# A pooling mixer's value and gate projections for groups 2 to 4 by seven block products, with weight sums made in DRAM

## What is computed

```python
def pool_mixer(h, w_in, w_grp, scale, w_out):
    v, gate = jnp.split(h @ w_in, 2, axis=-1)
    cs = jnp.cumsum(v32, axis=1)
    for g, w in enumerate(POOL_WINDOWS):          # windows 2, 4, 8, 16
        sl = slice(g * POOL_GROUP_DIM, (g + 1) * POOL_GROUP_DIM)
        ...
        groups.append((c - c_shift) / cnt - v32[..., sl])
    u = jnp.einsum('blgc,gcd->blgd', u, w_grp).reshape(b_, L, E_POOL) * scale
    return (u * jax.nn.silu(gate)) @ w_out
```

## Time and profile before

| | us |
|---|---|
| three runs: lowest, median, highest | 1538.06, 1538.21, 1538.75 |
| the profiled execution, its own time | 1539.07 |
| its span, first to last instruction | 1537.3 |
| PE busy | 1524.9 |
| DVE busy | 1049.2 |
| ACT busy | 577.6 |
| POOL busy | 362.9 |
| bytes moved by DMA | 170.75 MB |

### The profile page before, as it was taken

The page is one execution under the profiler, slowest core; times in us unless marked ns, Lnnn a source line. Parts: engine busy times, 40 slices in busy tenths (PEclk is TensorE's granted clock), DMA queues, the critical chain, the costliest instruction groups (busy, mean ns, idle before and its releaser), DMA issues.

```text
span 1537.3 us, 29781 instructions
## 1 busy us (share of the span) xinstructions
PE 1524.9 (99%) x12343; PEld 1366.5 (89%) x12343; DVE 1049.2 (68%) x1750; ACT 577.6 (38%) x1038; POOL 362.9 (24%) x333
## 2 busy tenths in 40 slices
PE   9999999999999999999999999999999999999998
PEld 9999999999998899889898898888888988888887
DVE  6656565765767678676887678779615787797246
ACT  5323222253344244434444445472112246541121
POOL 0000000030422134032332224434430044343510
PEclk9999999999999999999999999999999999999999
DMA  5322322323332324322334233554324335552331
GB/s 171 110 83 84 101 91 83 109 85 101 102 107 89 111 88 136 111 84 93 103 112 139 70 117 112 155 163 139 98 94 138 110 103 151 148 168 83 124 123 55
DMA packets 151859, 170.75 MB, mean 111 GB/s; under 512 B 6348, under 2 KB 122480, under 8 KB 151728
## 3 DMA queue, kind: packets, MB, share of 16 engines
q1 hardware_dynamic: 119728, 138.71, 29.0%
q10 hardware_dynamic: 31920, 29.97, 6.6%
q0 software_dynamic: 80, 0.20, 0.0%
HBM read 151.82 MB, written 17.04 MB: 110 GB/s over the span
## 4 chain that ended last, share of the span: by engine, by line
PE 48%; DVE 3%; ACT 0%; issue 0%; ACTq 0%
PE acc L415 13%; PE acc L416 13%; PE acc L417 13%; PE aux L417 1%; PE aux L416 1%; PE aux L415 1%; PE aux L1420 1%; DVE xns L2569 1%; PE aux L1438 1%; PE aux L1439 0%; PE aux L1386 0%; DVE yal L2559 0%; PE aux L643 0%; PE aux L645 0%; PE aux L576 0%
## 5 line engine op out<-in xcount | busy, mean ns | idle before, releaser
L415 PE MATMUL acc<-xhis,whi 128*128 128x264 f32 (+2 forms) x1848 | 608.9, 330 | 0.0
L417 PE MATMUL acc<-xhis,wlo 128*128 128x264 f32 (+2 forms) x1848 | 601.9, 326 | 0.0
L416 PE MATMUL acc<-xlos,whi 128*128 128x264 f32 (+2 forms) x1848 | 601.8, 326 | 0.0
L415 PEld LDWEIGHTS acc<-xhis,whi 128*128 128x128 f32 x1848 | 348.0, 188 | 29.8 <-issue 1.0
L417 PEld LDWEIGHTS acc<-xhis,wlo 128*128 128x128 f32 x1848 | 347.9, 188 | 29.3
L416 PEld LDWEIGHTS acc<-xlos,whi 128*128 128x128 f32 x1848 | 348.2, 188 | 27.1
L410 POOL TENSOR_TENSOR wlo<-raw,whi 128x1024 fp32r<-128x1024 f32 x84 | 208.5, 2483 | 366.0 <-DVE whi L2614 366.0
L406 ACT ACTIVATE whi<-raw 128x1024 fp32r<-128x1024 f32 x158 | 164.0, 1047 | 131.5 <-PE acc L417 119.3
L410 DVE TENSOR_TENSOR wlo<-raw,whi 128x1024 fp32r<-128x1024 f32 x81 | 99.8, 1235 | 36.9 <-ACT whi L406 36.7
L2292 DVE TENSOR_TENSOR wlo<-raw,whi 128x1024 fp32r<-128x1024 f32 x77 | 94.7, 1232 | 27.2 <-ACT whi L406 27.1
L2614 DVE CAST whi<-raw 128x1024 fp32r<-128x1024 f32 x84 | 61.2, 733 | 54.0 <-PE acc L417 53.8
(11 more groups left out here) (394 smaller groups left out, 2782.4 us busy)
## 6 DMA issues: line engine op xcount, KB each, us to landing
raw<-in_w_in SPq DMA_DIRECT2D x38, 1024.0 KB, 5.5
raw<-in_hgrn_w_in SPq DMA_DIRECT2D x32, 1024.0 KB, 5.9
raw<-in_pool_w_in SPq DMA_DIRECT2D x15, 1024.0 KB, 5.6
raw<-in_pool_w_out SPq DMA_DIRECT2D x8, 1024.0 KB, 4.9
raw<-in_hgrn_w_out SPq DMA_DIRECT2D x8, 1024.0 KB, 5.1
raw<-in_w_out SPq DMA_DIRECT2D x8, 1024.0 KB, 5.0
v_turn<-vb ACTq DMA_DIRECT2D x8, 544.0 KB, 2.7
raw<-in_pool_w_grp SPq DMA_DIRECT2D x4, 1024.0 KB, 5.3
```

Of the source, the lines that this page charges most:

```text
L415: pe.matmul(dst, stat[0], mov[0], start=first, stop=False)
L416: pe.matmul(dst, stat[0], mov[1], start=False, stop=False)
L417: return pe.matmul(dst, stat[1], mov[0], start=False, stop=last)
```

## The change

Groups 2 to 4 (G = 1 to 3) no longer make their four value and four gate units as such. Two units are taken together as a pair (p = 0, 1 the value pairs, p = 2, 3 the gate pairs). A pair's weight, 1024 x 256, is cut into four blocks of 512 x 128 (`d1`, `b12`, `d2`, `d3`), the input into four of 512 channels x 264 tokens. In place of the eight block products of a plain product there are seven, in Strassen's manner (Winograd's form): with `d1`, `d2`, `d3` and four sums of weight blocks, `t1 = d1 + b12`, `t3 = b12 + d3`, `t2 = d3 + t1`, `t4 = d2 + t2`. A block product is 4 tiles x 3 = 12 matmuls of 264 columns. Their results are accumulated in `aux`, `acc` and `aux2` and put together by small copies on ACT (`copied_sum`, 128 x 264, PSUM to `sqs`) and sums on DVE (`sum_11`, `sum_21`, `sums_2`, `scaled`).

- **Weight sums.** POOL issues, from its first us on, 8 DMAs per pair, DRAM to DRAM, 256 KB each: four copies, then four that accumulate, with a wait on `t_moved` after each of four steps. 12 pairs are made in 7 chains. SP waits for `t_moved` before it loads a chunk with such blocks.
- **Input sums.** Four sums of input blocks are made once: DVE's `s_sums` (8 operations, four times, after units 3 to 6 of group 1), split by ACT (`s_hi`) and DVE (`s_lo`).
- **Weight pieces.** For a pair there are 7 blocks of 128 x 512 to split, where there were 2 pieces of 128 x 1024. A `raw` chunk holds up to 4 blocks. `weight_blocks` makes the table of which block is split at which event, `weight_chunks` that of the loads.
- **Order.** In a group, the value pairs now come before the output units of the group before it; the gate pairs and the grp units come after these.

The core of the diff. The order of block products, and the chunks of weights:

```diff
+def strassen_order():
...
+    uses = []
+    for p in (0, 2):
+        uses += [(p, "d1"), (p, "d2"), (p, "t2"), (p, "t3"), (p, "d3"), (p, "t1")]
+        uses += [(p + 1, "d1"), (p + 1, "d2"), (p, "t4"), (p + 1, "t2"), (p + 1, "t3"), (p + 1, "d3"), (p + 1, "t1"),
+                 (p + 1, "t4")]
+    return uses
...
+def weight_chunks():
...
+    chunks = [("k8", 0, n) for n in range(4)] + [("k4", 0, 0)]
+    for G in range(1, NG):
+        chunks += [("blocks", G, (n, min(n + 4, 14))) for n in (0, 4, 8, 12)]
+        chunks += [("k4", G - 1, 1), ("k4", G - 1, 2)]
+        chunks += [("blocks", G, (n, min(n + 4, 28))) for n in (14, 18, 22, 26)] + [("k4", G, 0)]
+    return chunks + [("k4", NG - 1, 1), ("k4", NG - 1, 2)]
```

SP's waits before a chunk `c`:

```diff
+                    before, g, m = CHUNKS[c - RAW]
+                    if before == "blocks":
+                        wait_apart(sp, "sp", (sl_ready, N_USES * (g - 1) + m[1]))
+                    elif before == "k4":
+                        wait_apart(sp, "sp", (lo_ready, k4_piece(g, 2 * m + 2) + CREDIT))
...
+                if what == "blocks":
+                    sp.wait_ge(t_moved, T_MOVED[G, USES[n[1] - 1][0]])
```

POOL, right after its first memsets:

```diff
+            for G, pairs in T_CHAINS:
...
+                for p, (t1, t2, t3, t4) in zip(pairs, sums):
+                    pool.dma_start(t1, w_block(G, p, "d1")).then_inc(t_moved, 16)
+                    pool.dma_start(t3, w_block(G, p, "b12")).then_inc(t_moved, 16)
+                    pool.dma_start(t2, w_block(G, p, "d3")).then_inc(t_moved, 16)
+                    pool.dma_start(t4, w_block(G, p, "d2")).then_inc(t_moved, 16)
...
+                pool.wait_ge(t_moved, moved)
...
+                    pool.dma_start(t1, w_block(G, p, "b12"), accum_op=ALU.add).then_inc(t_moved, 16)
+                    pool.dma_start(t3, w_block(G, p, "d3"), accum_op=ALU.add).then_inc(t_moved, 16)
...
+                pool.wait_ge(t_moved, moved)
...
+                    pool.dma_start(t2, t1, accum_op=ALU.add, max_dma_last_dim=2048).then_inc(t_moved, 16)
...
+                pool.wait_ge(t_moved, moved)
...
+                    pool.dma_start(t4, t2, accum_op=ALU.add, max_dma_last_dim=2048).then_inc(t_moved, 16)
...
+                pool.wait_ge(t_moved, moved)
```

PE's order:

```diff
+            def two_units(G, p):
...
+                block_product(first, G, p, "d1", x_block(0, 0), True)
...
+                block_product(second, G, p, "d2", x_block(1, 0), True)
...
+                if p % 2:
+                    fourth_sum(G, p - 1)
...
+                pe.wait_ge(s_copied, 3 * t + 1)
+                block_product(first, G, p, "t2", s_block(1), False)
...
+                block_product(third, G, p, "t3", s_block(2), True)
...
+                pe.wait_ge(sum_done, summed(t, "11"))
...
+                block_product(second, G, p, "d3", s_block(3), True)
...
+                pe.wait_ge(s_copied, 3 * t + 2)
...
+                block_product(first, G, p, "t1", s_block(0), False)
...
+            for G in range(1, NG):
+                two_units(G, 0)
+                two_units(G, 1)
+                pe.wait_ge(sum_done, summed(4 * G - 3, "12"))
+                out_a_pair(G - 1)
+                fourth_sum(G, 1)
+                out_a(G - 1)
+                two_units(G, 2)
+                two_units(G, 3)
+                pe.wait_ge(sum_done, summed(4 * G - 2, "12"))
+                grp_a(G, 0)
+                fourth_sum(G, 3)
+                pe.wait_ge(sum_done, summed(4 * G - 1, "12"))
+                for n in range(1, GT):
+                    grp_a(G, n)
+            out_a_pair(NG - 1)
+            out_a(NG - 1)
```

DVE, the sums of input blocks, and their place in the loop over group 1's units:

```diff
+            def s_sums(k):
...
+                for half in range(2):
+                    dve.tensor_tensor(sq[half], xhi[:, 4 * half + k, :], xlo[:, 4 * half + k, :], ALU.add)\
+                       .then_inc(s_step, 1)
...
+                dve.tensor_tensor(s1, a22, a21, ALU.subtract).then_inc(s_step, 1)
+                dve.tensor_tensor(s2, a21, a22, ALU.subtract).then_inc(s_step, 1)
+                dve.tensor_tensor(s3, a11, a21, ALU.subtract).then_inc(s_step, 1)
+                dve.tensor_tensor(s4, a11, a12, ALU.subtract).then_inc(s_step, 1)
...
+                dve.tensor_tensor(s2, s2, a11, ALU.subtract).then_inc(s_step, 1)
+                dve.tensor_tensor(s4, s4, s1, ALU.add).then_inc(s_step, 1)
...
+                lows(("unit", u))
+                if 3 <= u < 7:
+                    s_sums(u - 3)
+                if 8 <= u < 12:
+                    s_lo(u - 8)
```

755 lines of the change are left out of this document (551 added, 204 removed).

## The result

| | before | changed |
|---|---|---|
| median of the runs (lowest, highest) | 1538.38 (1538.06, 1538.75), 4 runs | 1609.68 (1601.44, 1612.23), 4 runs |
| the profiled execution, its own time; its span | 1539.07; 1537.3 | 1601.44; 1598.9 |
| PE busy | 1524.9 | 1530.7 |

The ratio is 1.0451, with an interval of 1.0418 to 1.0484. The forecast was 1570, with a range of 1550 to 1600: the direction was right, the size was not, and the range did not hold it. The profiled execution is the fastest of the four, so the profile shows a loss of 61.6 us of span, and some 8 more are in the other executions, of which there is no trace.

A forecast was written before the change was run, and what follows sets the result against it. The prediction took PE's matmuls to bound the pooling mixer; 17.5 us saved against added waits, opening and contention gave +32.2 on 1539.07, 1571.3, or 1570 us beside the median, with a range of 1550 to 1600.

The forecast's parts named there:

- The pace, -17.5: Pooling mixer, PE: 144 matmuls fewer at 0.1213 us each, 17.5 us less, all on the path.
- Group 1, +9.8 and +3.9: Group 1: DVE's input sums delay evictions, PE loses 9.8 us; then t2 waits 3.9 us for ACT's copy of block 0.
- End of the value phase, +14.5: Groups 2 to 4, before output units: PE waits for sums_2 behind two landings in a row, 14.5 us.
- End of the gate phase, +6.9: Groups 2 to 4: PE's t4 of the fourth pair waits for sums behind the next group's first block, 6.9 us.
- start of the next value phase, +5.2: Groups 3 and 4: ACT's copy of the next block 0 comes 2.6 us after PE could use it, 5.2 us.
- last group, +1.4: Group 4: z_lo of the last grp unit stands behind a weight split, which the output units meet with 1.4 us.
- Opening, +2: Opening: POOL's first chain goes out beside the first inputs while PE waits for xt; 2 us, between nothing and 5.6.
- Contention, +6: 25 MB of sums until about group 4's end lengthen twelve landings on the path by 0.5 us each, 6 us.
- The clock: Rival: each of the five longest new waits brings 1.2 GHz for two block products, 14.5 us, 1585; chance 0.12.
- The loads keep up: Rival: weight chunks land before ACT asks, so the kernel is not slower, 1540 us or 1533; together 0.11.
- The sums come late: Rival: POOL's chains take 47 us, SP waits for t_moved, some 20 us over groups 3 and 4, 1590; chance 0.13.

The follow-up runs named there:

- small_s: Changed kernel with the input sums made over 8 or 16 columns instead of 264 or 528, every instruction kept: 1592.50 us.
- no_dma: Changed kernel without POOL's DMAs of weight sums, t1 to t4 loaded from plain weight blocks, no wait for t_moved: 1585.92 us.
- before_dma: Kernel before with POOL's 96 DMAs of weight sums added, whose results nobody uses or waits for: 1543.12 us.
- delay: Changed kernel with POOL's first chain sent after the input's last piece landed, and SP's t_moved wait naming the chunk's last pair with t blocks: 1595.48 us.
- holds: Kernel before with PE held up 18 times in groups 2 to 4 by waits for short POOL memsets: 1671.56 us.
- warm: Changed kernel with 24 matmuls on constants ahead of PE's wait before each group's first output pair: 1598.47 us.

## Why the prediction was right in direction and wrong in size

Step by step, with the terms as they were put.

**The pace, -17.5.** Holds: where the changed kernel has full clock and no wait, matmuls start 0.121 us apart as before, and there are 144 fewer.

**Group 1, +9.8 and +3.9.** The mechanism holds, the division doesn't. The sums took 3.55 us where 3.5 was worked out; the eviction behind them moved by 8.54, of which 5.0 is the opening. The first `pz` came 10.7 us late beyond the opening, but only 7.2 of these are waits of PE, less than forecast; 3.5 are slower matmuls, of which the forecast knew nothing. The last `pz`, forecast at 86.7, came at 91.7, which is exact beyond the opening's 5.0; as two errors met in it, that is partly luck. PE's wait for the first `t2` was 3.0, not 3.9. `small_s` gave 10 to 17 us back.

**End of the value phase, +14.5.** The mechanism holds row by row: copy behind `w_out` piece behind landing. It measured 21.5. Without the traffic it was 15.6 (`no_dma`), so the sum was right for landings without that traffic, and the landings with it were not.

**End of the gate phase, +6.9; start of the next value phase, +5.2; last group, +1.4.** The first was 9.6 with the traffic, 7.9 without; the two `t2` waits of groups 3 and 4 were 5.3 - 3.0 = 2.3, half of what was forecast; the grp units' waits for `zlos` 2.3. Another 5.2 us, for output units' evictions and the one without a releaser, have no term in the forecast.

**Opening, +2.** Mis-sized: 5.0 in the trace, and 4.4 alone (`before_dma`). The bound from above, 5.6, held. I had taken the low end on the argument that only four copies are out when PE waits. That was so, POOL issued the next step at 12.13 and PE's wait for `xt` ended at 12.34, but the four were enough: the wait grew by 3.4 us.

**Contention, +6.** Mis-sized too. I gave each of twelve landings 0.5 us. Between the profiled executions, up to the memset, the whole traffic is 15.0 us by `no_dma` and the opening's part 5.6 by `delay`, which leaves 9.4 for the landings behind it, where I had 6. The medians say 23.8 and 14.2 and leave the same; the 8 us more in both are the unexplained distance of the changed kernel's other executions. The median of the `w_out` landings grew by 1.0 us, and single ones by more: in group 2 a chunk was issued by 110.5 and ACT got it at 118.75, 8.3 us.

**The clock, nothing in the sum.** This is the step that failed. The forecast's waits came to 32.2 + 17.5 = 49.7 us; the new idle time is 54.8. Had the sum ended there it would have said 1576 for an execution that took 1601. (That the two sums of waits are so near is partly luck: the ends of the phases were too small in the forecast, group 1 and `t2` too large.) The missing 23.4 is PE's slower matmuls, 22.1 of them by the clock's record, and I had the clock as a rival at 0.12, because no row of the trace before showed a wait of 4 us or more. Even the rival was too small as put: it priced the five longest waits at 2.9 us each, 14.5. In fact `holds` shows 2.3 to 2.4 us for each wait of 4.80 us and more, and that waits of 2.48 us bring it in half of the cases. In the changed kernel's trace eleven of thirteen waits of over 1.5 us have a stretch of 0.50 within them or up to 1.4 us behind them, 2.0 us each. The rule of the Trainium skill ("TensorE: Matmul & The Clock Gate", Part 1), that the throttled clock is the default and only activity releases it, spoke for the rival, and the traces agree with it: the granted clock is 0.50 behind the waits in `holds`, and stays at 1.00 where `warm` keeps PE at work. With the 5.1 us that the waits were longer and the 23.4 of slower matmuls the sum would be 1571.3 + 5.1 + 23.4 = 1599.8, and that execution took 1601.4. The 8 us between it and the median stay open: other executions of the changed kernel may wait for longer landings, but none of them is in these rows.

The rivals otherwise. *The loads keep up* is refuted by ACT's 31.6 us of waits for `w_out`. *The sums come late* is refuted as well: POOL's DMAs of 512 rows followed each other by 0.61 to 0.65 us (once 0.77), not 2.8, so the issue is mostly a fixed cost, and the last of them went out at 253 us.

The other page that the prediction weighed, "DMA: Bandwidth & Descriptors" of the Trainium skill, gives its fit in the section on the anatomy of one DMA for DMAs that GpSimd issues; 4.4 us for 1 MB is my estimate from it. The loads in question are SP's, so the prediction used the fit outside of what the page states it for. Here it was 4.9 for `w_out` before, 5.2 in `no_dma` and 5.9 with the weight sums; the measured landings decide, and the estimate is below each of them.

## What to carry over

Sum the waits that a change brings to the engine on the path, and then add for each of them what the clock takes afterwards: here 2.3 to 2.4 us for each wait of 4.8 us and more and 1.7 us in half of the cases for one of 2.5 us, which made the difference between 2.4% and 4% in the profiled execution. A change that saves matmuls by giving other engines small, dependent work must leave slack at every handover, since a load that nobody waited for before turns all traffic, its own included, into time on the path. Traffic that costs little in one kernel (4.4 us here) is no measure of what it costs in another (15 to 24). And compare a trace with the time of its own execution first: the changed kernel's is 8 us off its median, as much as some of the effects read from it.

## What I had not expected of the hardware

- PE's granted clock falls to 0.50 late in a wait, at its end or shortly behind it and stays there for a while, so it is paid by the matmuls that follow: 33.8 us on 98.5 us of waits in `holds`, and hardly more for each wait of 8.3 us than for one of 4.8 (2.4 and 2.3). With the same waits each time, the runs agree within 0.3 us.
- DMAs that copy or accumulate from DRAM to DRAM, 256 KB each, landed in 5.9 us in the median (5.3 for sums of sums), and POOL issued them 0.52 to 0.65 us apart.
- Additions on POOL and splits on DVE lengthen each other when they meet: DVE's 1.22 us became 1.77 and once 4.38, POOL's 0.75 up to 1.80.
